# Two transformer blocks on one core: modulation columns by row sums, bias strips in two products, first block in another order

## What is computed

```python
mod = (jax.nn.silu(c) @ w_ada[l] + b_ada[l]).reshape(B, N_MOD, D)   # 9 vectors of 1024
m = [mod[:, j] for j in range(N_MOD)]
h = modulate(rmsnorm(x, ffn1_pre_g[l]), m[0], m[1])                  # h*(1+scale)+shift
y = swiglu(h, ffn1_w_gate[l], ffn1_w_up[l], ffn1_w_down[l])          # width 2816
x = x + 0.5 * m[2][:, None, :] * rmsnorm(y, ffn1_post_g[l])
h = modulate(rmsnorm(x, mix_pre_g[l]), m[3], m[4])
q, k, v, q_idx, k_idx, w_idx, x_lru, g_lru = split(h @ w_in[l])
attn = dsa_attention(q, k, v, q_idx, k_idx, w_idx, rel_bias)   # index scores pick 64 keys per query
lru = rg_lru_branch(x_lru, g_lru, ...)                         # conv(4), gates, linear recurrence, gelu gate
y = concatenate([rmsnorm(attn, attn_out_g[l]), rmsnorm(lru, lru_out_g[l])], -1) @ w_out[l]
x = x + m[5][:, None, :] * rmsnorm(y, mix_post_g[l])
h = modulate(rmsnorm(x, ffn2_pre_g[l]), m[6], m[7])
y = swiglu(h, ffn2_w_gate[l], ffn2_w_up[l], ffn2_w_down[l])
x = x + 0.5 * m[8][:, None, :] * rmsnorm(y, ffn2_post_g[l])
# then second_block: two layers of mixers and a PEER feed-forward that gathers expert rows
```

## Time and profile before

| | us |
|---|---|
| median of 3 runs | 2338.21 |
| lowest and highest | 2336.78, 2345.2 |
| the profiled execution | 2334.5 |
| its span, first to last instruction | 2332.6 |
| mean granted clock of the matrix engine | 0.951 of full |

### The profile page before, as it was taken

The page is one execution under the profiler, slowest core; times in us unless marked ns, Lnnn a source line. Parts: engine busy times, 40 slices in busy tenths (PEclk is TensorE's granted clock), DMA queues, the critical chain, the costliest instruction groups (busy, mean ns, idle before and its releaser), DMA issues.

```text
span 2332.6 us, 20377 instructions
## 1 busy us (share of the span) xinstructions
PE 2056.7 (88%) x6296; PEld 1114.9 (48%) x6296; DVE 1298.5 (56%) x3298; ACT 625.0 (27%) x1519; POOL 613.8 (26%) x554
## 2 busy tenths in 40 slices
PE   7998999799999759999988998997989898777886
PEld 4886478488844424444433443442444443333332
DVE  4533025410002346877567687657677776777764
ACT  2000013310001322254323236322324432222221
POOL 1100000000000023333334334334334334544442
PEclk9998989799999879999988999999999999999899
DMA  9976833344487469999999999999999999999998
GB/s 403 386 310 239 306 108 141 108 146 145 155 301 266 170 231 421 420 421 358 421 410 398 421 421 410 405 421 416 418 421 421 356 421 397 422 421 421 415 411 334
DMA packets 112877, 794.18 MB, mean 340 GB/s; under 512 B 12304, under 2 KB 15888, under 8 KB 17168
## 3 DMA queue, kind: packets, MB, share of 16 engines
q0 software_dynamic: 78912, 574.65, 60.2%
q1 hardware_dynamic: 28656, 207.63, 23.7%
q10 hardware_dynamic: 5216, 10.77, 1.3%
HBM read 788.29 MB, written 4.72 MB: 340 GB/s over the span
## 4 chain that ended last, share of the span: by engine, by line
PE 55%; DMA 22%; DVE 12%; ACT 5%; issue 4%; POOL 1%; POOLq 0%; DVEq 0%; ACTq 0%
DMA wide<-experts_in,pick_idx 21%; PE PS L941 16%; PE PS L1344 15%; PE PS L455 10%; PE PS L1405 8%; DVE wide L1008 4%; ACT diag L927 1%; DMA early<-ada_in 1%; POOL wide L1057 1%; PE PS L1372 1%; DVE topi L956 1%; DVE topi L959 1%; DVE topf L958 1%; PE PS L1452 1%; PE PS L693 1%
## 5 line engine op out<-in xcount | busy, mean ns | idle before, releaser
L941 PE MATMUL PS<-wide,diag 128*128 128x512 f32 x2048 | 1004.5, 630 | 212.0 <-ACT diag L927 205.6
L1057 POOL DMA_INDIRECT wide<-experts_in,pick_idx x512 | 585.8, 1144 | 1308.7 <-PE PS L941 789.2
L1008 DVE CUSTOM_DVE_ANT_0 wide<-wide,htok 128x1024 f32<-128x1024 f32 x512 | 619.9, 1224 | 271.1 <-DMA wide<-experts_in,pick_idx 264.7
L941 PEld LDWEIGHTS PS<-wide,diag 128*128 128x128 f32 x2048 | 391.3, 199 | 741.2 <-issue 418.5
L1344 PE MATMUL PS<-hT,ring 128*128 128x256 f32 x1744 | 382.0, 382 | 3.7 <-ACT hT L1141 3.7
L1344 PEld LDWEIGHTS PS<-hT,ring 128*128 128x128 f32 x1744 | 333.0, 191 | 51.5 <-issue 5.9
L455 PE MATMUL PS<-ring,hTm 128*128 128x512 f32 (+1 forms) x704 | 323.6, 589 | 2.1 <-ACT hTm L305 1.7
L927 ACT ACTIVATE diag<-cst,coef 128x128 f32<-128x128 f32 x512 | 177.6, 394 | 275.9 <-DVE coef L1019 271.5
L922 ACT ACTIVATE coef<-dots 128x2 f32<-128x2 f32 x256 | 52.2, 204 | 635.1 <-DVE dots L1008 634.5
L455 PEld LDWEIGHTS PS<-ring,hTm 128*128 128x128 f32 x704 | 134.0, 192 | 163.7 <-issue 154.3
L1405 PE MATMUL PS<-ring,actT 128*128 128x512 f32 x352 | 153.8, 598 | 0.9 <-DVE actT L1653 0.9
(11 more groups left out here) (316 smaller groups left out, 1395.3 us busy)
## 6 DMA issues: line engine op xcount, KB each, us to landing
ring<-wts_in SPq DMA_DIRECT2D x197, 1024.0 KB
early<-ada_in POOLq DMA_DIRECT2D x36, 1024.0 KB, 8.2
wide<-experts_in,pick_idx POOLq DMA_INDIRECT x512
strip_t<-scr ACTq DMA_DIRECT2D x1, 2048.0 KB, 13.7
strip_dil<-scr ACTq DMA_DIRECT2D x1, 1536.0 KB, 19.3
x<-x_in ACTq DMA_DIRECT2D x1, 1024.0 KB, 15.6
bias_t<-strip_t ACTq DMA_DIRECT2D x1, 1024.0 KB, 13.0
wrow<-norm_row_in ACTq DMA_DIRECT2D x2, 512.0 KB
```

What stands on the lines that cost most here:

```text
L941: last = pe.matmul(PS[:, ACC + half, :], diag[:, n % RING, :], ups[:, n % RING, half * BANK:(half + 1) * BANK], start=k == 0, stop=k == PI ...
L1008: v.tensor_tensor_reduce(out=downs[:, n % RING, :], in0=downs[:, n % RING, :], in1=htok[:, tb, :], scale=1.0, scalar=0.0, op0=ALU.mult, op ...
L1057: pool.indirect_dma_start(pairs_of_rows[:, k % RING, :, :].rearrange("p c n -> p (c n)"), None, experts.rearrange("l e d -> (l e) d"), bas ...
```

## The change

The modulation matrix is stored transposed. DVE now multiplies a row piece of it by silu(c), which is broadcast to all partitions (`cact`, 128 x 1024), and sums along the row in the same instruction (`chunk_of`). The sum is one column of a modulation vector, so 72 of these give all columns, and `column_sums` is gone. Three of them stand before each of the first products of gate_up, and the columns of vectors 2 to 8 are finished after product 18. The bias strips are two matmuls with 8 and 6 output partitions; their 14 rows are copied once and each row is repeated 128 times by the store. `down` may start with 20 of 22 products ready; one half's turn stands inside the down of the other; the value product is split by halves (the v tiles are loaded twice) and the second half's stands among the logits. The in-projection starts with the index queries and keys. The order of the constants' loads at the start changes too. The rest of the diff, not shown, is ACT's side of the same order, names and buffers.

```diff
-STREAM = [("gu1", "gu1", range(FT)), ("dn1", "dn1", [*range(FT // 2)] * TB), ("v1", "v1", range(2)), ("in1", "in1", range(11)),
-          ("out1", "out1", [2, 3, 0, 1] * TB), ("gu2", "gu2", range(FT)), ("dn2", "dn2", [*range(FT // 2)] * TB)]
+STREAM = [("gu1", "gu1", range(FT)), ("dn1", "dn1", [*range(FT // 2)] * TB), ("v1_0", "v1", range(2)), ("in1", "in1", range(9)),
+          ("v1_1", "v1", range(2)), ("in1b", "in1", range(9, 11)),
+          ("out1", "out1", [0, 1, 0, 1, 2, 3, 2, 3]), ("gu2", "gu2", range(FT)), ("dn2", "dn2", [*range(FT // 2)] * TB)]
...
-G_X, G_QI, G_KI, G_G, G_Q, G_K = 0, 4, 8, 9, 13, 14
+G_QI, G_KI, G_X, G_Q, G_K, G_G = 0, 4, 5, 9, 10, 17
...
@@ -1147,31 +1149,31 @@
                 act.wait_ge(m["rows_summed"], i + 1)
                 act.copy(rows[:, i, :], flat(PS[:, bank:bank + 2, :])).then_inc(m["rows_ready"], 1)
 
+            act.dma_start(cact[:, :], c_row.to_broadcast([P, D])).then_inc(m["c_loaded"], 16)
+            act.dma_start(x[:, :, :], x_in.rearrange("b (t p) d -> p (b t) d", p=P)).then_inc(m["x_loaded"], 16)
             act.dma_start(s1[:, :], small1).then_inc(m["smalls_loaded"], 16)
             act.dma_start(cst[:, :], consts).then_inc(m["consts_loaded"], 16)
-            act.dma_start(cst1[:, :], consts1).then_inc(m["strip_loaded"], 16)
-            act.dma_start(x[:, :, :], x_in.rearrange("b (t p) d -> p (b t) d", p=P)).then_inc(m["x_loaded"], 16)
-            act.dma_start(s2[:, :, :], small2).then_inc(m["smalls2_loaded"], 16)
-            act.dma_start(lbt[:, 0:4], lb_in).then_inc(m["smalls2_loaded"], 16)
...
+            act.wait_ge(m["c_loaded"], 16)
+            act.activation(cact[:, :], cact[:, :], ACT.Silu).then_inc(m["c_act"], 1)
             act.wait_ge(m["consts_loaded"], 16)
...
             for tb in range(TB):
                 pre(0, tb)
...
+            act.wait_ge(m["smalls_loaded"], 16)
+            act.wait_ge(m["mod_added"], 14)
+            act.dma_start(cst1[:, :], consts1).then_inc(m["strip_loaded"], 16)
+            act.dma_start(s2[:, :, :], small2).then_inc(m["smalls2_loaded"], 16)
+            act.dma_start(lbt[:, 0:4], lb_in).then_inc(m["smalls2_loaded"], 16)
             for tb in range(TB):
                 evacuate(0, tb)
+            act.wait_ge(m["strips_summed"], 2)
+            act.copy(scr1[0:HEADS, 0:BANK], PS[0:HEADS, 6, :]).then_inc(m["strips_copied"], 1)
+            act.copy(scr1[0:A2, BANK:2 * BANK], PS[0:A2, 7, :]).then_inc(m["strips_copied"], 1)
+            act.wait_ge(m["strips_copied"], 2)
+            for strip, heads, at in ((strip_t5, HEADS, 0), (strip_dil, A2, BANK)):
+                act.dma_start(strip.rearrange("p (h n) -> h p n", n=BANK),
+                              scr1[0:heads, at:at + BANK].unsqueeze(1).to_broadcast([heads, P, BANK]))\
+                    .then_inc(m["strips_stored"], 16)
...
+                    if tb == 0 and t in (0, 10):
+                        pe.wait_ge(m["act_ready"], FT * (f + 1) - (0 if t else 2))
...
+            pe.wait_ge(m["consts_loaded"], 16)
+            for tb in range(TB):
+                turn(0, tb)
             pe.wait_ge(m["smalls_loaded"], 16)
             pe.wait_ge(m["strip_loaded"], 16)
...
+            for bank, name, heads, rows_, hot in ((6, "rel", HEADS, 32, "t5"), (7, "rel2", A2, 33, "dil")):
+                pe.matmul(PS[0:heads, bank, :], o1(name, 0, heads, rows_), cst1[0:rows_, CC1[hot]:CC1[hot] + BANK],
+                          start=True, stop=True).then_inc(m["strips_summed"], 1)
...
-            gate_up(0, "gu1")
-            column_sums(2, 3, PS[:, 0, :])
-            down("dn1", 0, 0, 1)
+            gate_up(0)
+            down(0, 0, 0, 10)
             pe.wait_ge(m["post_cols"], 2)
+            pe.wait_ge(m["act_ready"], FT)
             gain_row(0, 2)
-            down("dn1", 0, 1, 11)
-            down("dn1", 1, 0, 11)
-            column_sums(3, 6, PS[:, 0, :])
-            pe.wait_ge(m["mod_read"], 3)
+            down(0, 0, 10, 11)
+            pe.wait_ge(m["strips_copied"], 2)
+            down(0, 1, 0, 8)
+            turn(1, 0)
+            down(0, 1, 8, 11)
+            pe.wait_ge(m["post_cols"], 3)
             pe.wait_ge(m["rows_ready"], 1)
-            for tb in range(TB):
-                turn(1, tb)
-
...
+            gain_row(1, 2)
...
+            index_weights(0)
+            values_of(0, 0, KC)
+            pe.wait_ge(m["rows_ready"], 2)
+            turn(1, 1)
+            hT_ready(1, 1)
...
-            pe.wait_ge(m["proj_copied"], 11)
+            pe.wait_ge(m["v_copied"], 1)
+            values_of(1, 0, 4)
+            pe.wait_ge(m["proj_copied"], 9)
             pe.wait_ge(m["idx_relu"], 3)
             logits(0, 8, 0, 2)
+            pe.wait_ge(m["lru_gates_sig"], 4)
+            logits(0, 4, 1, 6)
+            values_of(1, 4, KC)
+            proj(9)
...
             attn_turn(0)
+            pe.wait_ge(m["proj_copied"], 11)
+            pe.wait_ge(m["attn_by_scalar"], 1)
+            out_proj(0, 0)
+            pe.wait_ge(m["lru_sq"], 1)
+            chain(PS[:, 6, 0:S], [(C("ones"), scr1[:, 2048 + c * S:2048 + (c + 1) * S]) for c in range(4)])\
+                .then_inc(m["lru_sumsq"], 1)
+            attn_turn(1)
+            pe.wait_ge(m["attn_by_scalar"], 2)
+            out_proj(1, 0)
             pe.wait_ge(m["lru_merged"], 1)
-            out_proj(0, 0)
...
+            gate_up(1)
+            pe.wait_ge(m["rows_ready"], 3)
+            for tb in range(TB):
+                down(1, tb, 0, 11)
...
+            def chunk_of(j, n):
+                q, k = divmod(n, 2)
+                v.wait_ge(ada_loaded[q], j * 16 + 16)
+                w = ada_ring[:, q, k * D:(k + 1) * D]
+                v.tensor_tensor_reduce(out=w, in0=w, in1=cact[:, :], scale=1.0, scalar=0.0, op0=ALU.mult, op1=ALU.add,
+                                       accum_out=modr[:, 8 * j + n:8 * j + n + 1]).then_inc(m["mod_added"], 1)
...
+            def columns(j0, j1):
+                v.wait_ge(m["mod_added"], 8 * j1)
+                V(v.tensor_tensor(modc[:, 8 * j0:8 * j1], modr[:, 8 * j0:8 * j1], o1("b_ada", 8 * j0, 8 * (j1 - j0)), ALU.add))
+
             v.wait_ge(m["c_act"], 1)
-            vector_of(0, rows[:, 0, :])
-            vector_of(1, rows[:, 1, :])
+            for n in range(8):
+                chunk_of(0, n)
             v.wait_ge(m["x_loaded"], 16)
...
+            for n in range(8):
+                chunk_of(1, n)
+            v.wait_ge(m["smalls_loaded"], 16)
+            columns(0, 2)
             pre_columns(0)
             v.sem_inc(m["post_cols"], 1)
...
+            for k in range(FT):
+                for c in range(16 + 3 * k, min(19 + 3 * k, 8 * N_MOD)):
+                    chunk_of(c // 8, c % 8)
+                ffn_tile(0, k % 4, k // 4)
+                if k == 18:
+                    columns(2, N_MOD)
+                    for i in range(3):
+                        post_columns(i)
+                        if i:
+                            pre_columns(i)
+                    v.sem_inc(m["post_cols"], 3)
             post(0, 0, 4)
             normalize(1, 0)
+            evacuate(1, 0)
...
+            conv(0)
             v.wait_ge(m["v_copied"], 1)
             index(0)
+            for c in range(1, 4):
+                conv(c)
+            v.wait_ge(m["mask_ready"], 1)
+            index(1)
             v.wait_ge(m["lru_decay"], 8)
             t, i_, xc, tmp = scr1[:, 1024:2048], scr1[:, 2048:3072], scr1[:, 0:1024], flat(actT[:, G_X:G_X + 4, :])
             V.go(v.tensor_tensor(i_, i_, xc, ALU.mult))
             V(v.tensor_scalar(tmp, t, 1.0, None, ALU.add))
             V(v.reciprocal(tmp, tmp))
             v.scalar_tensor_tensor(t, t, 2.0, tmp, ALU.mult, ALU.mult).then_inc(m["lru_mult_in"], 1)
-            v.wait_ge(m["mask_ready"], 1)
...
-            v.wait_ge(m["probs_T"], 1)
-            maxima(0, 4, 1, 2, 2)
-            maxima(4, 8, 1, 0, 3)
+            maxima(0, 4, 1, 6, 2)
+            maxima(4, 8, 1, 6, 3)
             attended(0)
+            attn_norm(0)
+            v.wait_ge(m["lru_gelu"], 1)
+            v.tensor_tensor(xc, xc, flat(actT[:, G_G:G_G + 4, :]), ALU.mult).then_inc(m["lru_out"], 1)
+            attended(1)
+            attn_norm(1)
```

309 lines of the change are left out of this document (105 added, 204 removed).

## The result

The changed kernel takes **2361.7 us** (median of four runs, 2360.2 to 2363.0), the kernel before 2337.5 us in the same comparison: a ratio of 1.0097 with a 95% interval of 1.0073 to 1.0121. It is 1% slower. The prediction was 2354 us, in a range of 2288 to 2372. The profiled execution took 2361.0 us, with a span of 2359.3 against 2332.6 us before.

The account below looks back on a forecast made before the run. TensorE, busy 88% of the span, was taken as the bound, so gains come from gaps or removed matmuls. Terms −3.7 +2 +58.5 +3 −15.2 −15.2 −10.9 −2.7 give +15.8: 2350.3 profiled, 2354 us as median; range 2288 to 2372.

Parts of the forecast that it names:

- the rival "as quick as before": Strip store in gate_up 1 lands in 19.3 us, no stall, all gains count: 2292 us, chance 0.2.
- b, the store: Strips in two products, stored from 8 and 6 partitions: store 80 us, PE stands 58.5 us in gate_up 1.
- the text's own flip: Store time above which the changed kernel turns slower than the one before: 64 us.
- The upper bound of 140 us: Strip store at a rate set by its partitions, 26 GB/s for 8 of 128: 140 us, kernel 2414 us.
- the second rival: Strip store priced by its 2 KB pieces: 40 us with landing, stall 18.5, kernel 2314 us, chance 0.15.
- The clock: Slow PE clock in gate_up 1: 2 us at its start, about 3 us behind the stall.
- a, the start: Start of the kernel: gate_up 1 begins at 45.4 instead of 49.1, 3.7 us earlier.
- c: End of gate_up 1: wait of 9.6, column sums 3.58 and 2.0 of slow clock gone, −15.2 us.
- d: From down 1 to the first in-projection tile: 14.6 us instead of 29.8, −15.2 us.
- e: In-projection to gate_up 2: 150 us instead of 160.9, −10.9 us, ends −4 and −17.
- f: Second down: no wait for last products, gain row hidden in a wait, −2.7 us.
- the likeliest case: Strip store takes 70 to 95 us, kernel 2342 to 2370 us, chance 0.57.

Follow-up runs that it names:

- +64: Changed kernel with half of each store read from second copies on partitions 64 and up, on SP's queue: 2328.6 us in one run.
- +32: Changed kernel with half of each store read from second copies on partitions 32 and up, on SP's queue: 2371.3 us in one run.
- the last experiment: Kernel with stores from 128 and 96 partitions, with strip products, stores and bias loads moved behind gate_up 1 and the one-hot table loaded last: 2288.4 us.
- the spread kernel: Changed kernel with 16 copies of each strip row, stored from 128 and 96 partitions instead of 8 and 6: 2292.1 us.

## Why the prediction was right, step by step

- **The mechanism and the verdict.** The forecast was a stall of PE some 30 us after the first gate_up pass, ended by ACT's silu behind the wait for the stores. PE's 128 passes ended 29.7 us after the start (predicted 29.7), and the wait moved or the store spread, the stall was gone and the time fell to 2288 and 2292 us, which is the 2292 of the rival "as quick as before".
- **b, the store.** It took 90.1 us (50.31 to 140.39) where 80 were taken, so the stall was 68.1 instead of 58.5; this is the largest miss. 80 was only the middle of two far bounds, 19.3 and 140; its reasons, that nothing in the trace spoke for a free concentration on 8 partitions and that the stores share a queue, give no number. That it came within 10 us of the measured time is luck, and the forecast of a slower kernel hung on it, since the text's own flip lies at 64 us. The runs put ports in its place: four heads of both strips on one port are 2.1 MB, which at the 25 GB/s of the tail is an estimated 84 us. The sentence beside the sum had 77, from a port rate of 27. The upper bound of 140 us, a rate for each partition, was a wrong picture: +64 and +32 would have had to be equal. The price of the second rival came near only where the pieces are spread over ports: 37.3 us measured four partitions apart, 40 worked out, and 84 ns a piece against its 93.
- **The clock.** 2.0 us on the first four tiles as predicted (29.74 against 27.7), 2.4 behind the stall (126.98 for 576 passes against 124.58 in the kernel with ACT's wait moved) where 3 were taken.
- **a, the start.** 48.54 where 45.4 was predicted: of 3.7 us of gain 0.6 came. The row sums were done at 34.0, earlier than the 36.6 worked out. But the one-hot table landed 12.95 us after its issue, not 9.2 (1.3 us later in all), and the two products took 3.67 us, not 1.8: the row of 14 passes was read as 14 products, and each product is two passes. A term was mis-sized by a misread count. Loading the table earlier did not pay (2298.9 us); the last experiment, which takes its load and the products off the path ahead of gate_up, moved the boundaries by 5 us.
- **c.** Down follows gate_up without a gap (273.41), the wait of 9.6 and the column sums are gone. Row sums did catch up after the stall, as was assumed; nothing was late next.
- **d.** From the last pass of down (351.60) to the first in-projection tile (364.62) 13.0 us, predicted 14.6 (its terms add up to 14.4). The turn inside down was put at nothing, as hidden, but PE has no gap in down to hide it in: it took 0.87 us, and down 78.2 (273.41 to 351.60), 0.9 more than the 77.3 that the text implies. **e.** 150.4 us, predicted 150; no wait of 15 us. The split of PE and DVE work in it was less exact than the sum looks: the index order has a slack of about 3 us, and the value product covers little. **f.** -2.2, predicted -2.7.
- **Sum.** Stall, clock and start missed by +9.6, -0.6 and +3.1, d, e and f by -1.6, +0.4 and +0.5, and the turn inside down by +0.9; the second block gave back 1.6, which no term held and which is within its scatter. The profiled run came out at 2361.0 against 2350.3 worked out for it. The 3.7 us between profile and median did not recur: 2361.0 against 2361.7. 2361.7 lies in the likeliest case's own range of 2342 to 2370.
- **The sign.** The text put the flip at a store of 64 us. The runs bracket it widely: 49.2 us gave 2329, slightly faster than before, and 85.6 us 2371, one run each.

## What to carry to other kernels

A DMA that leaves from a few neighbouring partitions had the rate of one or two ports here, 25 or 49 GB/s, on one queue and on two: fewer matmuls and copies are a bad trade if they gather its source, and 16 copies of each row come almost free from the same two matmuls (3.99 us against 3.67). Look for the wait that stands ahead of an engine's main loop in its instruction order: a transfer with six microseconds of cover was harmless there, and the cheapest cure is to put the wait where its result is first used. When a change pulls one transfer forward, ask which one it delays; the early table moved the start of gate_up by 5 us and gate_up took 11.6 longer.

## What the runs showed of the hardware that was not expected

**Issue time.** The second of two stores from few partitions held ACT for 8.4 us in the changed kernel and 23.0 us in the kernel before with two products, 4.9 with the partitions four apart and 0.60 from 128 and 96 partitions. For an engine with compute behind the DMA in its order this is a cost of its own. What it depends on was not tried.

**The granted clock behind attention.** Nearly the same instructions (the first in-projection tile starts at 294.84 in one kernel and at 295.54 in the other) ran at different clocks over the same 32 us. In the views by stretch the spread kernel is first, the kernel with ACT's wait moved second:

```profile
380.00:412.00 32.00, 29.22 (x141) 21.92 (x139) 5.95 (x18) 17.31 (x41) 0.00 (x0) 0.84 0.32 105
```

```profile
380.00:412.00 32.00, 27.99 (x149) 20.87 (x148) 7.51 (x19) 19.63 (x49) 0.00 (x0) 1.00 0.38 139
```

The first 16 passes of the out-projection took 9.13 us in the one and 7.11 in the other, and gate_up 2 came 4 us later in its stage. The changed kernel shows 0.84 too. Why one of them kept the full level is open. It may be an accident of the execution: of that kernel's four runs the slowest, 2297.4 us, has a mean clock of 0.955 and the others 0.963 to 0.969. It is the size of the difference between their medians, so that difference should not be read as a merit of either order.
